# A hybrid decoder step: cached values weighted under each key block's own maximum, factors in the fold, decoding delta states moved into the last heads

## The reference, cut to what matters

```python
gate = einsum('bhqd,bhnd->bhqn', q, kmean)        # kmean: mean key of each block
_, sel = lax.top_k(gate, 3)
s = where(mask, einsum(q, k) * scale, -inf)       # kept blocks and own token
p = softmax(s)
o = einsum(p, v)
```

```python
v_new = beta * (v - exp(g) * (k @ S));  S = exp(g) * S + outer(k, v_new);  o = q @ S
```

## Time and profile before

| | |
|---|---|
| median of 3 runs | 591.93 us (591.51 to 597.29) |
| the profiled execution | 592.36 us, its span 590.6 us |
| mean granted clock of TensorE | 0.945 |
| busy: PE, PEld, DVE, ACT, POOL | 91%, 76%, 59%, 28%, 9% |
| moved | 116.53 MB, mean 197 GB/s |

### The profile page before, as it was taken

One profiled execution on the slowest core, in us unless ns is written; L12 is line 12 of the kernel. 1 busy time (PEld: TensorE's weight loads), 2 busy tenths in 40 slices (PEclk: granted clock), 3 DMA queues, 4 the chain that ended last, 5 costly groups with the idle time before them and its releaser, 6 DMA issues.

```text
span 590.6 us, 10244 instructions
## 1 busy us (share of the span) xinstructions
PE 536.5 (91%) x3943; PEld 450.6 (76%) x3943; DVE 350.1 (59%) x550; ACT 164.4 (28%) x233; POOL 55.7 (9%) x125
## 2 busy tenths in 40 slices
PE   7889999897997889888699689888999999999997
PEld 6567767674796767666464169688999999999996
DVE  4441578576987979854753556555664665555441
ACT  4102114512033212221001133462434343423420
POOL 6800000000107500000101000000000000000000
PEclk8879998996799999999888799997999999999999
DMA  9996574294087658462569997684556564545201
GB/s 292 339 306 199 175 248 156 73 246 162 19 273 246 220 175 283 148 205 84 180 215 378 369 321 234 213 267 144 166 192 191 166 198 146 192 155 185 74 18 38
DMA packets 98919, 116.53 MB, mean 197 GB/s; under 512 B 6301, under 2 KB 81262, under 8 KB 98854
## 3 DMA queue, kind: packets, MB, share of 16 engines
q1 hardware_dynamic: 93218, 104.42, 55.3%
q10 hardware_dynamic: 3908, 7.42, 3.5%
q0 software_dynamic: 1744, 4.04, 2.6%
HBM read 113.04 MB, written 2.99 MB: 196 GB/s over the span
## 4 chain that ended last, share of the span: by engine, by line
PE 68%; DVE 19%; DMA 6%; ACT 3%; issue 2%; ACTq 1%; DVEq 0%
PE bank L336 64%; DVE prod L943 4%; DVE s_all L1063 4%; DVE mats L943 3%; DMA ring<-in_ada_w_dram 2%; DMA ring<-in_w_out_dram 2%; DVE BTP L943 1%; DVE cv L1171 1%; DMA ring<-in_cache_v_dram 1%; DMA x_nat<-in_x_sample_dram 1%; PE bank L373 1%; ACT w_part L1752 1%; PE bank L382 1%; PE bank L544 1%; DVE w_ab L943 0%
## 5 line engine op out<-in xcount | busy, mean ns | idle before, releaser
L336 PE MATMUL bank<-a_hi,w_part 128*128 128x264 f32 x832 | 154.4, 287 | 2.1 <-DVE a_lo L1508 2.1
L943 DVE TENSOR_TENSOR w_part<-ring,w_part 128x2048 fp32r<-128x2048 f32 (+1 forms) x38 | 84.9, 2236 | 90.2 <-ACT w_part L1752 90.2
L336 PEld LDWEIGHTS bank<-a_hi,w_part 128*128 128x128 f32 x832 | 130.6, 191 | 2.6 <-issue 2.6
L336 PE MATMUL bank<-a_lo,w_part 128*128 128x264 f32 x416 | 118.9, 286 | 0.0
L1752 ACT ACTIVATE w_part<-ring 128x2048 fp32r<-128x2048 f32 (+1 forms) x38 | 70.9, 1871 | 86.9 <-PE bank L336 75.0
L336 PE MATMUL bank<-hT,ring 128*128 128x264 f32 x352 | 84.3, 398 | 1.8 <-ACT proj L1599 1.8
L336 PEld LDWEIGHTS bank<-hT,ring 128*128 128x128 f32 x352 | 67.7, 195 | 16.1 <-issue 4.5
L336 PEld LDWEIGHTS bank<-a_lo,w_part 128*128 128x128 f32 x416 | 79.5, 191 | 0.1
L336 PE MATMUL bank<-hid_hi,w_part 128*128 128x264 f32 x352 | 64.9, 285 | 0.0
L336 PEld LDWEIGHTS bank<-hid_hi,w_part 128*128 128x128 f32 x352 | 54.5, 188 | 0.1
L336 PEld LDWEIGHTS bank<-ident 128*128 128x128 f32 x344 | 47.3, 219 | 9.3 <-issue 5.6
(11 more groups left out here) (333 smaller groups left out, 576.4 us busy)
## 6 DMA issues: line engine op xcount, KB each, us to landing
ring<-in_ada_w_dram SPq DMA_DIRECT2D x24, 1024.0 KB, 7.1
ring<-in_cache_k_dram SPq DMA_DIRECT2D x64, 256.0 KB, 3.7
ring<-in_w_in_dram SPq DMA_DIRECT2D x11, 1024.0 KB, 5.4
ring<-in_w_gate_dram SPq DMA_DIRECT2D x11, 1024.0 KB, 5.3
ring<-in_w_up_dram SPq DMA_DIRECT2D x11, 1024.0 KB, 5.3
ring<-in_cache_v_dram SPq DMA_DIRECT2D x40, 256.0 KB, 4.3
ring<-in_w_down_dram SPq DMA_DIRECT2D x8, 1024.0 KB, 5.1
ring<-in_cache_v_dram ACTq DMA_DIRECT2D x24, 256.0 KB, 5.2
```

The costliest lines, as they stand in the source:

```text
L336: return pe.matmul(out, lhsT, rhs, start=start, stop=stop, skip_group_check=True)
L943: return v.tensor_tensor(out, a, b_, op)
```

## The change

It computes the same function. Its parts:

- Page numbers: a value item now holds one page of each of the four blocks (`PPB * k + hf`), so that the four partition groups of a bank are the four blocks. All four pages of each item are issued by SP; ScalarE issues none.
- Each page's scores are shifted by the maximum of their own block (`top4`), and the exponentials go unscaled into the operand of the page products, for four sequences at a time (`G0`, `DMAX0`; `G1`, `DMAX1`; the two halves of `s_all`). The products of four sequences add up in one bank; a bank is copied once, by ScalarE.
- The ranking (`RK`: the smallest of four blocks is dropped, ties by index), the factors between the blocks' maxima and the shared one, and the denominators (`DEN`) are computed while pages are multiplied. The factors come in at the end: `WC` turns them into columns, `FO` multiplies them in with 16 products.
- `OWN`, `XA` and `XB` stand between heads 6 and 7 and the prompt's `UB` to `UD`; `XC` before the pages. `A9`, with its two ada loads, stands between `V6` and `V7` instead of before `V0`.
- Warm-up products: heads 6 and 7 have 10 and 4 in place of 18 and 6; those of `OWN`, `DMAX`, `DEXP`, `V0` and `VE` go, `FO` has 6.

```diff
@@ order
-             "... M6 POOL H5 UA A7 K15 H6 UB UC H7 UD A8 HE OWN "
-             "A9 DMAX DEXP V0 XA V1 XB V2 XC V3 XD V4 MX V5 V6 MW0 V7 VE MD MW1").split()
+             "... M6 POOL H5 UA A7 G0 K15 H6 DMAX0 OWN UB XA UC H7 XB UD A8 "
+             "HE XC G1 V0 DMAX1 V1 RK V2 XD V3 V4 DEN MX V5 V6 A9 V7 WC FO MW0 MD MW1").split()
@@ load_pages
-            first = q * NPG + hf * PGI
-            pages = [eng.value_load(table[0:1, first + k:first + k + 1], min_val=0, max_val=NPHYS - 1) for k in part]
+            index = [q * NPG + (PPB * k + hf if kind == "v" else hf * PGI + k) for k in part]
+            pages = [eng.value_load(table[0:1, n:n + 1], min_val=0, max_val=NPHYS - 1) for n in index]
@@ att_turn
-                for _ in range((14, 8, 2, 16, 4, 4, 18, 6)[h]):
+                for _ in range((14, 8, 2, 16, 4, 4, 10, 4)[h]):
@@ TensorE
+            def group_sums(g):
+                pe.wait_ge(sem("k_scored"), GS * (g + 1))
+                b = opened(f"gsT{g}", (3, 6)[g])
+                for n in range(2):
+                    o = g * GW + n * P
+                    pe.transpose(b[:, GW + n * P:GW + (n + 1) * P], s_all[:, o:o + P], ident[:, :])
+                closed(mm(b[:, 0:GW], ones[:, :], s_all[:, g * GW:(g + 1) * GW]), f"gsT{g}")
...
             def page_values(q):
+                g, j = q // GS, q % GS
+                if j == 0:
+                    pe.wait_ge(sem("p_ready"), g + 1)
+                    opened(f"pv{g}", (7, 4)[g])
+                b = bank[(7, 4)[g]]
                 for hf in range(HALVES):
                     slot = arrived(pe, ("v", (q, hf))).rearrange("p (k n) -> p k n", k=PGI)
+                    for k in range(NB):
+                        last = mm(b[32 * k:32 * k + 32, :], pP[g][:, j * NPG + PPB * k + hf, :], slot[:, k, :],
+                                  j + hf == 0, j == GS - 1 and hf == HALVES - 1)
...
+            def fold():
+                keep_awake(6, 6)
+                pe.wait_ge(sem("selw"), 1)
+                pe.wait_ge(sem("pv_rows"), 2)
+                b = opened("y8", 6)
+                for g in range(2):
+                    for c in range(AC):
+                        for h2 in range(2):
+                            r = 64 * h2
+                            last = mm(b[r:r + 64, c * NS + g * GS:c * NS + (g + 1) * GS],
+                                      pv_out[g][:, c * P + r:c * P + r + 64], selw[:, g, 2 * c + h2, :])
+                closed(last, "y8")
@@ VectorE
+            def group_sums(g):
+                if g == 0:
+                    v.wait_ge(sem("tails_out"), 64)
+                b = full(v, f"gsT{g}")
+                step(v.tensor_reduce(tokmax[:, 2 * g:2 * g + 2], b[:, GW:2 * GW].rearrange("p (n t) -> p n t", n=2), AX, ALU.max))
+                for n in range(2):
+                    o = g * GW + n * P
+                    last = v.tensor_scalar(w_a[:, o:o + P], ident[:, :], tokmax[:, 2 * g + n:2 * g + n + 1], None, ALU.mult)
+                inc(last, "max_diag")
+                freed(v.tensor_reduce(of(gate4, g), b[:, 0:GW].rearrange("p (n t h) -> p n h t", t=PPB, h=H), AX, ALU.add),
+                      f"gsT{g}")
+
+            def spread_max(g):
+                b = full(v, f"pmax{g}")
+                freed(v.tensor_reduce(of(top4, g), b[:, 0:GW].rearrange("p (n t h) -> p n h t", t=PPB, h=H), AX, ALU.max),
+                      f"pmax{g}")
...
+                s = paged(s_all[:, g * GW:(g + 1) * GW])
+                inc(tt(s, s, bc(of(top4, g).unsqueeze(2), [P, GS * NB, PPB, H]), ALU.subtract), "shifted")
...
+            def block_ranks(_):
...
+                step(v.tensor_reduce(low, over_blocks(gate4[:, :, :, :]), AX, ALU.min))
+                step(tt(cnt4[:, :, :, :], gate4[:, :, :, :], bc(low.unsqueeze(2), wide), ALU.is_le))
+                step(tt(cnt4[:, :, :, :], cnt4[:, :, :, :], bc(bidx[:, :, :].unsqueeze(1), wide), ALU.mult))
+                step(v.tensor_reduce(low, over_blocks(cnt4[:, :, :, :]), AX, ALU.max))
+                step(tt(gate4[:, :, :, :], cnt4[:, :, :, :], bc(low.unsqueeze(2), wide), ALU.is_lt))
...
+            def fold(_):
...
+                b = full(v, "y8")
+                freed(tt(mixT[:, PCH:PCH + AC, T:NT], b[:, 0:AC * NS].rearrange("p (c q) -> p c q", c=AC), own_v, ALU.add), "y8")
@@ ScalarE
+            def page_exps(g):
+                a.wait_ge(sem("shifted"), g + 1)
+                a.wait_ge(sem("p_zeroed"), g + 1)
+                s = s_all[:, g * GW:(g + 1) * GW].rearrange("p (j n h) -> p j n h", n=NPG, h=H)
+                inc(a.activation(p_own[g], s, ACT.Exp, scale=SCALE), "p_ready")
...
+            def pv_rows(q):
+                if q % GS == GS - 1:
+                    take(f"pv{q // GS}", pv_out[q // GS], P, AW, "pv_rows")
...
-            def value_pages(q):
...
-                        load_pages(a, item, range(PGI // 2, PGI))
@@ GpSimd
+            g.wait_ge(sem("krow_out"), 32)
+            step(g.memset(stg_p[:, :], 0.0))
+            g.sem_inc(sem("p_zeroed"), 1)
             spread_query(7)
-            g.wait_ge(sem("max_diag"), 1)
-            step(g.memset(prod[:, :], 0.0))
+            g.wait_ge(sem("k_scored"), NS)
+            step(g.memset(prod[:, 0:GS * XW], 0.0))
             g.sem_inc(sem("p_zeroed"), 1)
@@ SP
-                    load_pages(sp, it, range(PGI // 2 if kind == "v" and i[0] >= 2 else PGI))
+                    load_pages(sp, it, range(PGI))
```

More of the change, by code:

```diff
@@ L742, in own_scores @@
                 closed(mm(b[:, 0:NS * H], ones[0:NS, :], own8[:, 1, :]), "own")
[L743 to L772, removed]
@@ L785, in page_values @@
+                    if j < GS - 1 or hf < HALVES - 1:
                         used_up(last, ("v", (q, hf)), "pe_read")
[L786 to L799, removed]
+                if j == GS - 1:
+                    closed(last, f"pv{g}")
+                    read_by(f"pv{g}", ("v", (q, HALVES - 1)))
@@ new lines, in denominators, with turn_weights @@
+            def denominators():
+                pe.wait_ge(sem("p_ready"), 2)
+                b = opened("den", 6)
+                for g in range(2):
+                    last = mm(b[:, g * GW:(g + 1) * GW], ones[:, :], p_own[g])
+                closed(last, "den")
+            def turn_weights():
+                pe.wait_ge(sem("wgt"), 1)
+                b = opened("wcol", 5)
+                for g in range(2):
+                    last = mm(b[:, g:g + 1], w_a[:, g * P:(g + 1) * P], ident[:, 0:1])
+                closed(last, "wcol")
@@ L1377, in own_scores @@
-                step(v.tensor_scalar(g4, c4, float(min(TOPK, NB + 1)), None, ALU.is_lt))
-                step(v.tensor_scalar(c4, g4, FAR, -FAR, ALU.mult, ALU.add))
-                b = full(v, "sT")
-                freed(v.tensor_reduce(tokmax[:, :], b[:, :].rearrange("p (n t) -> p n t", n=4), AX, ALU.max), "sT")
-                v.wait_ge(bank_free[4], frees_at("sT"))
-                v.wait_ge(sem("tails_out"), 64)
-                for n in range(4):
-                    last = v.tensor_scalar(w_a[:, n * P:(n + 1) * P], ident[:, :], tokmax[:, n:n + 1], None, ALU.mult)
@@ new lines, in block_weights @@
+                step(tt(cnt4[:, :, :, :], cnt4[:, :, :, :], gate4[:, :, :, :], ALU.mult))
+                step(tt(sum4, sum4, cnt4[:, :, :, :], ALU.mult))
+                step(v.tensor_reduce(den, over_blocks(sum4), AX, ALU.add))
+                step(tt(den, den, own_e, ALU.add))
+                step(v.reciprocal(den, den))
+                tt(own_w, own_e, den, ALU.mult)
+                for g in range(2):
+                    q = slice(g * GS, (g + 1) * GS)
+                    last = tt(w_a[:, g * P:(g + 1) * P].rearrange("p (n j h) -> p j n h", n=NB, h=H), cnt4[:, q, :, :],
+                              bc(sm64[:, 4, q, :].unsqueeze(2), [P, GS, NB, H]), ALU.mult)
@@ new lines, in block_weights, with turn_weights @@
+                inc(last, "wgt")
+            def turn_weights(_):
+                b = full(v, "wcol")
+                every = [P, 2, H * GS]
+                freed(tt(selw[:, :, :, :].rearrange("p g h j -> p g (h j)"),
+                         bc(selq[:, :, :].rearrange("p h j -> p (h j)").unsqueeze(1), every),
+                         bc(b[:, 0:2].unsqueeze(2), every), ALU.mult), "wcol")
+                v.wait_ge(bank_free[5], frees_at("wcol"))
+                v.sem_inc(sem("selw"), 1)
@@ L1852, in _ @@
             step(g.memset(blk[:, :], 0.0))
-            step(g.memset(selc[:, :, :], 0.0))
-            step(g.memset(dm8[:, :], 0.0))
+            step(g.memset(selq[:, :, :], 0.0))
+            for n in range(NB):
+                step(g.memset(bidx[:, n, :], float(n + 1)))
             step(g.memset(i64[:, :], 0.0))
```

170 lines of the change are left out of this document (69 added, 101 removed).

## The result

| | before | after |
|---|---|---|
| median | 593.09 us, 4 runs (591.51 to 597.29) | 611.13 us, 4 runs (608.26 to 614.35) |
| ratio of the times | | 1.0294 [1.0212, 1.0377] |
| the profiled execution | 592.36 us | 608.26 us, its span 606.2 us |
| mean granted clock | 0.945 | 0.907 |
| first W_out product | 350.56 | 366.28 |

The change makes the kernel slower by 2.9%, 17.4 us on 593.09. Slower was forecast, but 598.4 us (592.5 to 604), so the time is outside the range. The two profiled executions differ by 15.9 us, and the first W_out product by 15.7: nothing behind it moved.

A forecast was written before the change was run, and what follows sets the result against it. TensorE-bound on average, but value-page loads limit the changed stretch: first page 290.5 + 55.0 + 6.8 + 4.8 = 357.1 against 350.6, +6.5; 592.36 + 6.5 - 0.4 = 598.4 us, range 592.5 to 604.

The forecast's parts named there:

- Part 2: Page loads by SP alone, 4.3 to 4.35 us an item; W_out slot 0 issued 55.0 us after the first page.
- full rate: Rival: pages flow at 376 GB/s under SP alone, W_out starts 5 to 8 us earlier, 584 to 587 us; chance 0.08.
- The front at full clock: Stretch up to A8's first weight product without clock loss: moved work starts A8 13.1 us later, at 286.4.
- Part 1: Stretch up to A8's first weight slot: A8 13.1 us later plus 2.5 for the clock, first page at 290.5.
- The clock of the front: TensorE's idle gaps around heads 6 and 7 halve its clock: +2.5 us taken, between 0 and 4.7.
- The page stretch: From SP's first page behind A8 to the issue of W_out slot 0: 55.0 us.
- Slots are free in time: Page ring: TensorE frees slots before SP needs them, with V0 done within 10 us of the first page.
- The landing: W_out slot 0 from issue to arrival, behind A9's loads and the last pages: 6.8 us.
- The tail: From slot 0's landing to the first W_out product: 4.8 us, set by the split, down from 9.9.
- signs I had named for being wrong: Page steps under 3 us, A8 starting before 283, or the fold coming after the split.
- The worse rival: TensorE enters the tail at half clock, another +2 to +6 us, 601 to 605 us; chance 0.12.
- What was taken at nothing: Ranking and denominators, about 5 and 4 us on VectorE in the page stretch, and other small moved work: 0 us.

The follow-up runs named there:

- e9_rank_late: e6_delta_back_act with the ranking RK moved from ahead of XB to behind V4: 591.99 us, ratio 0.9974.
- e10_rank_late_warm: e9_rank_late with 18 and 6 warm-up products in heads 6 and 7, 8 ahead of OWN and 14 ahead of XC: 592.53 us, ratio 0.9904.
- e6_delta_back_act: Kernel after, with OWN and the decoding delta steps put back and ScalarE issuing two of four pages per value item from sequence 2: 590.58 us, ratio 0.9962.

## Why the prediction was right in direction and wrong in size

- **SP's items (Part 2, right in kind).** 4.28 us an item in the middle, 241 GB/s, none of the 376, the rival "full rate" gone. Three edits confirm it: ScalarE's share back (-2.2%), taken from the old kernel (+2.4%), the table loads gone (-2.0%).
- **The front at full clock (Part 1, right within 1 us).** I had A8 13.1 us later by the moved work; with the clock mostly held up it is 14.1. K15's delay was +2.1 by the forecast and 2.1 measured (A7 to K15 6.10 against 4.04 us).
- **The clock of the front (Part 1, the step that failed).** I took +2.5 us between 0 and 4.7; it is 6.1. I doubled head 6, head 7 and XB, and left XA's one-column products at 3.27 us, because the only row showed them at full clock and I let the clock come back between the two gaps. It stayed at 0.50 for 18 us: XA alone cost 2.5 more. The Trainium skill, "TensorE: Matmul & The Clock Gate", "The HAM clock gate", has the clock fall after idling and return after busy work. The fall is as there. The return came late: not with 7.47 of 9 us busy from 275 to 284, but behind a stretch without a gap (3.40 of 3.40 us busy from 286.8 to 290.2, clock 0.71). By that sentence I had put the term near 4.7, and the trace shows more. First page DMA: forecast 290.5, measured 294.26, **+3.8**: the clock 3.6, the moved work 1.0, less 0.5 as A7 started earlier in this execution and 0.3 from A8 to the page.
- **The page stretch, first page to slot 0 (mis-sized).** Forecast 55.0, measured 58.5, **+3.5**. The first two steps were 5.15 and 5.45 us, then 4.28 to 4.66: +2.3 to v(6,1). "Slots are free in time" was wrong once: SP had the registers of the third item at 304.0, and V0, late and at half clock, released its slot at 304.7. The greater part is that single instructions of SP were slower: a table load took 0.97 us and a DMA 0.79. The stretch with A9's loads and the last items was 12.9 for 11.6; in it an ada load took 0.97 us to issue and a page 1.20 where others take 0.33. Why was not tested. The table loads of the second item in the view of L260 (ns min/median/max), and two DMAs in SP's timeline, of the kernel after:

```profile
L260 SPq TENSOR_LOAD <-table x4: 272/336/974, 296.2 to 298.7; - x4
...
300.44 0.79 SPq L265 DMA_DIRECT2D ring<-in_cache_v_dram  x1
...
345.70 1.20 SPq L265 DMA_DIRECT2D ring<-in_cache_v_dram  x1
```

- **The landing (mis-sized).** 8.3 us from issue to cast for 6.8: **+1.5**.
- **The tail.** 5.2 for 4.8: **+0.4**. It fell from 10.0, as forecast, but the fold's sum (363.39) was last by 0.4 us over the cast (362.96), as V7 and the turn of the factors ran at half clock. That is one of the signs I had named for being wrong, by a small amount.
- These four (first page, page stretch, landing, tail) make 9.2 us, which is the whole difference between 357.1 and 366.28. The rest of the 12.7 us of miss: the median of the kernel after stands 2.9 us above its profiled execution, where I had taken off 0.4, and behind the first W_out product 0.2 were added.
- **The worse rival** (half clock in the tail, chance 0.12) named the right cause in the wrong place: the front paid 6.1 us for the clock and the tail 0.4. In other orders it came true: e9_rank_late and e10_rank_late_warm went through the tail at half clock, with 24 warm-up records in 4.78 and 4.53 us for 2.94.
- **What was taken at nothing.** Ranking and denominators cost nothing in the kernel after: from 304.86 to 342.33 its chain is SP's. With ScalarE's share the ranking held the delta chain (e6_delta_back_act), 3.6 us of wait, though moving it did not change the time.

So the numbers part (own maxima, factors in the fold) costs no time: with the issue shared, the delta steps back, the ranking late and the split first the kernel beats the one before. What made the change slow are two things around it: all pages on SP (2.2%), and the delta steps ahead of A8 (1.0294 to 1.0108, 1.8%), part of it clock, as warm-up products win back 6 us of the front and, on top of ScalarE's share, 0.8%.

## What to carry to other kernels

Where pages come through a table, read the issuer's timeline from one item to the next, register loads included: that period, not bandwidth, may bound the stretch. A second issuer lifted it here; loading the registers earlier was not tried. Work that is moved ahead of a load's release delays every load behind it; work that sat in waits for loads was free here as long as no load's release hung on it. Price small products at half clock when an idle gap stands ahead of them, and after each cure look for the next wait in the order of the engine that ends last.

## What the runs showed of the hardware

- 32 fp32 products of one column (64 records) take 3.27 us at 2.4 GHz and 5.78 to 5.79 at 1.2 GHz: even these, which move next to no data, follow the clock.
- SP needs 0.27 us for a load from the page table, 0.55 with its register work, and 0.52 from one DMA to the next: four of each are 4.28 us. Single ones took up to 0.97 and 1.20 us.
- The granted clock stayed at 0.50 from 266 to 284 us while TensorE was busy 13.6 of 18 us, in pieces with gaps of 1.5 to 2.5 us. In e9_rank_late it stood at 0.50 from 338.5 to 348.5 us with TensorE busy all of the 10 us by its records, behind 12 us in which it was busy 8.05 and the clock 0.76:

```profile
326.00:338.00 12.00, 8.05 (x63) 2.22 (x56) 7.26 (x17) 2.96 (x4) 0.00 (x0) 0.76 1.06 364
338.50:348.50 10.00, 10.00 (x73) 8.89 (x66) 3.85 (x7) 5.64 (x5) 0.00 (x0) 0.50 1.10 349
```
